# A one-layer stick-breaking trunk in fp32: other homes for three buffers, another order of stores and loads, and long operations cut and spread

## What is computed

```python
def swiglu_ffn(u, w_in, w_out):                    # w_in 1024 x 5632, w_out 2816 x 1024
    gate, up = jnp.split(u @ w_in, 2, axis=-1)
    return (jax.nn.silu(gate) * up) @ w_out

h = h + 0.5 * swiglu_ffn(rmsnorm(h, ffn1_norm), ffn1_w_in, ffn1_w_out)
h = h + stick_breaking_attention(rmsnorm(h, mix_norm), sb_w_qkv, sb_w_o, valid)   # 8 heads of 128
h = h + 0.5 * swiglu_ffn(rmsnorm(h, ffn2_norm), ffn2_w_in, ffn2_w_out)
# then a final RMSNorm; the meta tokens are dropped
```

## Time and profile before

| | |
|---|---|
| median of 3 runs | 2029.91 us (2026.12 to 2030.18) |
| profiled execution: time, span | 2026.75 us, 2024.8 us |
| mean granted TensorE clock | 0.983 |
| PE busy | 1918.0 us (95%) |
| DVE busy | 1296.4 us (64%) |
| POOL busy | 1059.1 us (52%) |
| ACT busy | 756.6 us (37%) |
| HBM | 273.56 MB moved, 135 GB/s on the mean |

### The profile page before, as it was taken

The page is one execution under the profiler, slowest core; times in us unless marked ns, Lnnn a source line. Parts: engine busy times, 40 slices in busy tenths (PEclk is TensorE's granted clock), DMA queues, the critical chain, the costliest instruction groups (busy, mean ns, idle before and its releaser), DMA issues.

```text
span 2024.8 us, 37347 instructions
## 1 busy us (share of the span) xinstructions
PE 1918.0 (95%) x12508; PEld 1749.1 (86%) x12508; DVE 1296.4 (64%) x1751; ACT 756.6 (37%) x1495; POOL 1059.1 (52%) x998
## 2 busy tenths in 40 slices
PE   7899999999899988999989999989999999979997
PEld 6899999998899988999989987767887887768876
DVE  5866666665566758433379970296666766556675
ACT  5433433333222235222267761243343343322222
POOL 4355655564455535545377662345656566545560
PEclk9999999999899999999999999999999999989999
DMA  3234443446777411333322212014353435577732
GB/s 126 67 122 159 144 152 119 165 139 225 244 245 244 137 43 48 101 103 108 102 84 85 72 53 62 21 32 137 133 166 135 155 126 175 193 264 250 247 127 94
DMA packets 244611, 273.56 MB, mean 135 GB/s; under 512 B 12976, under 2 KB 176816, under 8 KB 244544
## 3 DMA queue, kind: packets, MB, share of 16 engines
q1 hardware_dynamic: 244544, 272.69, 40.8%
HBM read 179.58 MB, written 93.06 MB: 135 GB/s over the span
## 4 chain that ended last, share of the span: by engine, by line
PE 67%; issue 12%; POOL 9%; DVE 6%; DMA 2%; ACT 2%; SPq 1%; POOLq 0%; DVEq 0%; ACTq 0%
PE psum L1787 21%; PE psum L1789 21%; PE psum L1788 21%; POOL arena L703 7%; PE psum L1814 2%; POOL scratch L777 1%; DMA hidden<-scratch 1%; PE psum L2017 1%; DVE arena L1646 1%; DVE scratch L1755 1%; POOL arena L719 1%; DVE arena L1346 0%; DMA scratch<-w_o_dram 0%; DVE scratch L1399 0%; DVE arena L1632 0%
## 5 line engine op out<-in xcount | busy, mean ns | idle before, releaser
L1787 PE MATMUL psum<-arena 128*128 128x260 f32 (+3 forms) x3908 | 1252.7, 321 | 72.5 <-DVE scratch L1541 28.3
L1789 PE MATMUL psum<-arena 128*128 128x260 f32 (+3 forms) x3908 | 1233.6, 316 | 0.0
L1788 PE MATMUL psum<-arena 128*128 128x260 f32 (+3 forms) x3908 | 1231.4, 315 | 0.0
L1787 PEld LDWEIGHTS psum<-arena 128*128 128x128 f32 x3908 | 743.9, 190 | 134.2 <-issue 32.8
L1788 PEld LDWEIGHTS psum<-arena 128*128 128x128 f32 x3908 | 743.1, 190 | 45.4 <-issue 3.5
L1789 PEld LDWEIGHTS psum<-arena 128*128 128x128 f32 x3908 | 743.1, 190 | 44.2
L703 POOL TENSOR_TENSOR arena<-scratch,arena 128x512 fp32r<-128x512 f32 x365 | 506.3, 1408 | 483.7 <-ACT arena L937 483.6
L1399 DVE TENSOR_TENSOR scratch<-scratch 128x512 f32<-128x512 f32 x200 | 238.9, 1194 | 149.5 <-POOL arena L703 143.9
L794 POOL TENSOR_TENSOR arena<-scratch,arena 128x256 fp32r<-128x256 f32 x280 | 209.7, 767 | 210.5 <-ACT arena L1143 210.4
L937 ACT ACTIVATE arena<-scratch 128x512 fp32r<-128x512 f32 x371 | 215.2, 622 | 269.8 <-DVE scratch L1399 80.8
L1396 DVE TENSOR_TENSOR scratch<-scratch,psum 128x520 f32<-128x520 f32 (+1 forms) x265 | 182.5, 689 | 201.4 <-PE psum L1789 176.1
(11 more groups left out here) (93 smaller groups left out, 1315.0 us busy)
## 6 DMA issues: line engine op xcount, KB each, us to landing
scratch<-w_in_dram SPq DMA_DIRECT2D x88, 512.0 KB, 4.9
pairs<-scratch SPq DMA_DIRECT2D x140, 260.0 KB, 2.7
arena<-pairs SPq DMA_DIRECT2D x35, 1040.0 KB, 8.4
pairs<-scratch SPq DMA_DIRECT2D x140, 256.0 KB, 2.6
arena<-pairs SPq DMA_DIRECT2D x35, 1024.0 KB, 8.6
scratch<-w_out_dram SPq DMA_DIRECT2D x80, 256.0 KB, 3.1
qkv<-scratch SPq DMA_DIRECT2D x48, 260.0 KB, 2.1
scratch<-w_qkv_dram SPq DMA_DIRECT2D x24, 512.0 KB, 4.5
```

What stands on the lines that cost most here:

```text
L1787: nc.tensor.matmul(dst, wh, xh, start=start, stop=False, skip_group_check=True)
L1788: nc.tensor.matmul(dst, wh, xl, start=False, stop=False, skip_group_check=True)
L1789: return nc.tensor.matmul(dst, wl, xh, start=False, stop=stop, skip_group_check=True)
```

## The change

Six edits, made for both FFN stages:

1. `store_high` (T3, T2) becomes part of `store_second` and goes ahead of the low parts of B22 and B21. For the last pair the weights of down unit 1 are loaded between them, and all of `store_second` stands ahead of the loads of the rooms.
2. `sums_b[3]` lives in x2 instead of u0, x2 moves to the end of the scratch buffer (clear of raw_d and raw_h), and its clear stands behind the last unit's c22 add, with no wait for a store. PE waits for the last SiLU (`silu0`) before the down projection.
3. GpSimd makes the low parts of T3 and T2 right behind weight 3's and ahead of weight 0's, and T4's behind weight 6's, instead of all three ahead of weight 6's.
4. The two long splits of the plain turn are four operations each.
5. The common sums are added to the quadrants later: sum 0 behind the last group's unit 1, sum 1 behind unit 2, sums 2 and 3 between the shares of the plain turn.
6. QKV's squares live in c22 and u0, and its two early weights are copied ahead of the second half's squares.

```diff
-        sq_half = [piece(scratch, 4112, 2, HALF[n]) for n in range(3)]
+        sq_half = [(c22, u0) if n == QKV else (g0, g1) for n in range(3)]
-        x1, x2, x3, r0, r1 = (scratch[:, 5672 + 520 * j:5672 + 520 * (j + 1)] for j in range(5))
+        x1, x3, r0, r1, x2 = (scratch[:, 5672 + 520 * j:5672 + 520 * (j + 1)] for j in range(5))
-        sums_b = (xy, g0, g1, u0)
+        sums_b = (xy, g0, g1, x2)
...
-            def store_second(n, pair):
+            def store_second(n, pair, last=False):
                 store_part(n, "B21", pair, 0, x1, pair_hi, hi + 3, stored_second)
                 store_part(n, "B22", pair, 0, x2, pair_hi, hi + 4, stored_second)
+                store_part(n, "T3", pair, 0, g1, pair_hi, hi + 5, stored_high)
+                store_part(n, "T2", pair, 0, g0, pair_hi, hi + 6, stored_high)
+                if last:
+                    sp_eng.wait_ge(ffns[n]["w_loaded"], 32 * UNITS[n] + 32)
+                    load_down_weights(n, 1, 0, 1, 1)
                 store_part(n, "B22", pair, 1, c22, pair_lo, lo + 3, stored_second)
                 store_part(n, "B21", pair, 1, u0, pair_lo, lo + 4, stored_second)
...
-                store_second(n, HIDDEN_PAIRS - 1)
+                store_second(n, HIDDEN_PAIRS - 1, last=True)
                 room_free(1)
                 load_pairs(n, 0, 0, (0, 1))
-                store_high(n, HIDDEN_PAIRS - 1)
                 room_free(2)
                 load_pairs(n, 0, 0, (2, 3))
                 store_rest(n, HIDDEN_PAIRS - 1)
-                sp_eng.wait_ge(s["w_loaded"], 32 * UNITS[n] + 32)
-                load_down_weights(n, 1, 0, 1, 1)
...
                     for at, v in enumerate((3, 0, 6, 1, 2, 4, 5)):
-                        if at == 2 and pair is not None:
-                            pair_rows_lo(n, pair)
                         weight_lo(n, v, PRODUCTS * u + 6 + at)
+                        if pair is not None and at in (0, 2):
+                            pair_rows_lo(n, pair, (0, 1) if at == 0 else (2,))
...
-                nc.gpsimd.tensor_tensor(hid[n][1][:, :, 0:2 * half], raw_h[:, :, 0:2 * half],
-                                        hid[n][0][:, :, 0:2 * half].bitcast(F32), ALU.subtract)\
-                    .then_inc(s["h_lo"], 1)
+                for ft in range(2):
+                    for late in range(2):
+                        at = slice(late * half, (late + 1) * half)
+                        nc.gpsimd.tensor_tensor(hid[n][1][:, ft, at], raw_h[:, ft, at],
+                                                hid[n][0][:, ft, at].bitcast(F32), ALU.subtract).then_inc(s["h_lo"], 1)
...
                     add(c22, c22, "c", "c22")
                     if last:
+
+                        clear(sums_b[3], taken)
                         mix_down(n, 0, 0)
...
-                        dve.wait_ge(s["stored"], 48)
-                        clear(sums_b[3], taken)
...
+            def add_common(n, d, quarters):
+
+                dve.wait_ge(taken, TAKEN_ALL * (n // 2) + SUMS_CLEARED + PRODUCTS * (DOWN_UNITS - HK + d + 1))
+                for far, late in quarters:
+                    rows_of = quarter(n, d, far, late)
+                    nc.vector.tensor_tensor(rows_of, sums_b[d][:, 0:HALF[n]], rows_of, ALU.add).then_inc(sums_added, 1)
+
+            def common_among(n, at):
+
+                if at in (1, 3):
+                    add_common(n, 2 + at // 2, [(1, 0)])
+                elif at in (8, 10, 12, 14) if n == FFN1 else at in (4, 5, 6, 7):
+                    i = at // 2 - 4 if n == FFN1 else at - 4
+                    add_common(n, 2 + i // 2, [(i % 2, 1)])
...
-                if final:
-                    dve.wait_ge(taken, front + PRODUCTS)
-                    for at in ((1, 1), (1, 0), (0, 1)):
-                        nc.vector.tensor_tensor(quarter[at], common, quarter[at], ALU.add).then_inc(sums_added, 1)
...
                 for d in range(HK):
-                    down_unit(n, DOWN_UNITS - HK + d, d, final=True, more=d < HK - 1)
-                dve.wait_ge(sums_added, SUMS_ALL * (n // 2 + 1))
+                    down_unit(n, DOWN_UNITS - HK + d, d, more=d < HK - 1)
+                    if d in (1, 2):
+                        add_common(n, d - 1, ((1, 1), (1, 0), (0, 1)))
...
             def down_units(n):
+                pe.wait_ge(ffns[n]["silu0"], UNITS[n])
```

More of the change, by code:

```diff
@@ L767, in units, with pair_rows_lo @@
                     unit(UNITS[n] - 2)
-            def pair_rows_lo(n, pair):
+            def pair_rows_lo(n, pair, which=range(3)):
                 half, hi = HALF[n], HI_ALL * (n // 2) + 7 * pair
-                for at, (raw, high) in enumerate(((r1, g1), (r0, g0), (x3, x1))):
+                for at in which:
+                    raw, high = ((r1, g1), (r0, g0), (x3, x1))[at]
                     if at == 1:
@@ L921, in norm_halves @@
                             split_rows(n, 0)
-                        if (n, c, at) == (FFN2, 1, KT - 2):
+                        if (n, c, at) in ((QKV, 1, 0), (FFN2, 1, KT - 2)):
                             early_weights(n)
@@ L1573, in mix_down_last, with quarter, common_before, down_unit @@
                 nc.vector.tensor_tensor(s4_b, a12, s2_b, ALU.subtract).then_inc(s["mixed"], 1)
-            def down_unit(n, u, d, final=False, more=True):
+            def quarter(n, d, far, late):
+                return h[:, d + HK * far, late * HALF[n]:(late + 1) * HALF[n]]
+            def add_common(n, d, quarters):
[9 more added lines that the diff above has]
+                    add_common(n, 2 + i // 2, [(i % 2, 1)])
+            def common_before(n, at):
+                front = SUMS_ALL * (n // 2) + 1
+                if at == 6:
+                    dve.wait_ge(sums_added, front + 8)
+                elif at == (16 if n == FFN1 else 8):
+                    dve.wait_ge(sums_added, front + 12)
+            def down_unit(n, u, d, more=True):
                 s, half = ffns[n], HALF[n]
                 front = TAKEN_ALL * (n // 2) + SUMS_CLEARED + PRODUCTS * u
-                quarter = {(far, late): h[:, d + HK * far, late * half:(late + 1) * half]
-                           for far in range(2) for late in range(2)}
                 common = sums_b[d][:, 0:half]
@@ L1762, in last_turn @@
                     at, dt = q // KT * BANK, q % KT
+                    common_before(FFN2, q)
                     dve.wait_ge(s["down"], q + 1)
```

41 lines of the change are left out of this document (21 added, 20 removed).

## The result

The changed kernel has a median of 2016.84 us over 6 runs (2012.44 to 2021.52), the kernel before 2029.83 over 6 (2026.12 to 2032.34): a ratio of 0.9945, interval 0.9928 to 0.9962. It is faster by 13 us, not by the 33 forecast, and lies outside the range of 1988 to 2009.

A forecast was written before the change was run, and what follows sets the result against it. PE, busy 95% of the span, was taken to bound the kernel, so only its stands and half clock could be won. Gains of 31.2 off the profiled 2026.75 gave 1995.6, put at 1997 us, range 1988 to 2009.

The forecast's parts named there:

- FFN1, down projection begins: FFN1's first down unit: the clear stops waiting for a store and rooms land sooner, gain 9.2 us, bounds 4 to 12.
- FFN2, the same: FFN2's first down unit: the same rearrangement, with loads 2% smaller, ends it sooner, gain 8.1 us, bounds 3 to 11.
- last groups, both: Last group of both FFNs: VectorE's mixes and the take come sooner, gain 7.0 us together, bounds 2 to 9.
- FFN1's plain turn: FFN1's plain turn: single adds between the shares replace three adds that made PE stand, gain 4.7 us, bounds 2 to 5.
- FFN2's loop, nine turns: FFN2's loop: weight 6's wait of 0.99 goes, 0.75 comes back before product 5, gain 2.2 us over nine turns.
- FFN1's loop: FFN1's loop: the later stores still leave room before product 5 and the moved low part is harmless, gain 0.
- bound of -4: FFN2's loop, lower bound over nine turns: a loss of 4 us if the second stores land 0.7 later still.
- D: Rival, chance 0.04: in both loops the second stores land 5.2 us later, 59 lost against 29 won, 2057.
- A: Rival, chance 0.14: rooms land as before, down projections' beginnings gain only 4 and 3 us, 2006.
- B: Rival, chance 0.12: FFN2's loop gains its full 0.99 us a turn because the second stores land in time, 1989.
- C: Rival, chance 0.07: VectorE's mixes get in only behind GpSimd's last split piece, so the last groups keep their waits, 2003.
- E: Rival, chance 0.03: the whole change's gains are given back behind the next shared wait, 2026.

The follow-up runs named there:

- e7: Changed kernel with the loops' old store and GpSimd orders back, and one long GpSimd operation for each plain-turn split instead of four: 2003.66 us.
- e2: Changed kernel with GpSimd's old order of low parts back in the loops, stores kept in the new order: 10.5 us won against the changed kernel.
- e5: Changed kernel with the loops' old store order; GpSimd makes T3's and T2's low parts behind weight 0's again, T4's still behind weight 6's: 1995.35 us.
- e1: Changed kernel with the old order of the stores back in the loops, GpSimd's new order kept: 2010.69 us.
- e12: e1 with a semaphore of its own for the store of B22's low part, which alone VectorE's add into c22 then awaits: 1996.61 us.
- e4: e1 with T4's low part made by GpSimd only behind weight 4's of the next unit, instead of right behind weight 6's: 2005.70 us.
- e10: e5 with a semaphore of its own for the store of B22's low part, which alone VectorE's add into c22 then awaits: won nothing.

## Why the prediction missed

**Right.** By the table, taking FFN2's loop as nine turns (9/8 of the eight measured, and the ninth taken out of the stretch with the down projection's beginning):

```
term                              predicted   measured
FFN1, down projection begins            9.2        8.9
FFN2, the same                          8.1        8.0
last groups, both                       7.0        7.0
FFN1's plain turn                       4.7        3.7
FFN2's loop, nine turns                +2.2      -10.5
FFN1's loop                               0       -6.4
everything else                           0       -1.6
sum                                    31.2        9.1
```

The steps behind the first three hold: waits for clears gave way to waits for rooms of up to 3.4 (forecast "longest about 4"), and the take is late by 0.50 instead of 1.1. That the last groups come out at exactly 7.0 is in part luck: FFN1 gained 3.7 instead of 3.2, FFN2 3.3 instead of 3.8, and the prediction's own terms for FFN2 (3.0 + 1.6 - 1.1) give 3.5. The plain turn gained 1 us less than forecast, and the clock accounts for it: it fell behind an unchanged stand for the squares, which it did not before. In e7 it held behind the same stand (3.05 us), and the plain turn took 37.5 instead of 39.0.

**The step that failed** is in the part on FFN2's loop: "It will wait 0.75 to 0.8, and product 6 not at all. Gain 0.99 - 0.75 = 0.24, times nine". The wait of 0.75 to 0.8 came as forecast (0.80), and so did the delay of VectorE's add behind it: 1.4 forecast, 1.45 measured. Part of that agreement is luck, since GpSimd's early low parts have a share in both; with the stores' order alone (e2) the delay is 1.28 and the wait 0.68. But the working stopped at products 5 and 6. The wait for weight 6 had been giving VectorE's mixes their time, and the c12 chain behind them had 0.2 us of room. e5 shows what its removal is worth even where no store moves, 0.3 a turn instead of 0.99. With the stores and the early low parts on top PE waited 1.22 there in each turn, and the turn became 1.17 longer where the forecast had it 0.24 shorter. The bound of -4 for this term was therefore too narrow: it knew only the stores' delay at w. The term came to -10.5.

**FFN1's loop, "0",** failed by the same step, and measured -6.4. The working compared the stores' landing with the moment at which product 5 needs w, where there was room in all turns but one, and never with the mixes. And it set GpSimd's moved low parts at nothing, though two of them lie beside VectorE's differences and the third beside its mixes. That order alone costs 2.7 in this stretch (e1, 430.2 against 427.5) and the stores' alone 3.0 (e2). In e12, where the add no longer waits for B21's store, the stretch is back at 427.6 with GpSimd's order as in the change.

**The rivals.** D had the right place, the second stores, and the wrong size: VectorE's add came 1.45 later, not 5.2. Its price of 59 came from the whole time of a store. A, B and C are ruled out: the beginnings gained in full, the loop gained nothing, the last groups gained 7.0. E named what happened in the loop, a gain that is given back behind the next wait, but for the whole change (2026); outside the loops only 1 us was given back.

The prediction used the sharing of VectorE and GpSimd for the last group, where the mix of 3.48 lies beside the split of 5.21, and not for the loops. The page "SBUF — State Buffer" of the Trainium skill, in "SBUF: two separate sides", states it as a rule: a VectorE instruction with two inputs in SBUF shuts out a GpSimd instruction that reads SBUF, or the other way round, whichever starts first, for its whole length. The trace agrees: 0.68 became 1.78 beside a low part of 1.83, and the mix of e7 ended 0.3 behind the split of 4.65.

How the 1.2 at c12 divides among its causes stays open in part. The changed kernel's mixes take 4.25, as e1's do, and e4 shows 1.0 less without the third low part beside them. But freeing the add of B21's store (e12) takes 0.6 off the same wait with that part in place, so the two are not terms that add up.

## What to carry to other kernels

When a wait of PE is to be removed, follow the unit to its end and into the next one, and write down the room of each later meeting, not only of the next; here the following one had 0.2 us, and 0.86 of a wait of 1.00 came back there. An instruction moved on GpSimd cost time on VectorE here where it came to lie beside an operation that reads two tiles in SBUF (0.68 became 1.78), so look for what lies beside it in its new place, and for which store or semaphore hangs on that. And where an engine waits for a count of several stores, let it wait only for the one that reads the buffer it writes: that was worth 14 us in e12, though nothing in e10, where the freed instructions ran into GpSimd's.

## What the hardware showed that was not expected

- The clock behind a stand of the same length differs between executions: 3.03 us at 739.44 was followed by 3.4 us at 0.50, 3.06 at 750.6 before and 3.05 in e7 by 1.00.
- One VectorE operation of 0.4 to 0.5 us lasted 4.58 beside one GpSimd operation of 4.65; cut into four, the same work let each mix in after 1.4.
- The first 250 matmuls took 47.8 to 49.8 us over these kernels, which do the same work there. A stage is better compared from its own first matmul than from the program's start.
